# A streaming encoder step with 32 experts: two expert matrices lie over x while the experts run

## The chip, the cores and the metric

The kernel runs on one core of one Trainium2 chip. The metric is the device time of one launch in microseconds, as the median of several runs; lower is better.

## The reference

One layer of an encoder for 576 tokens of width 1024 (512 prompt rows, 64 sample rows), all in float32. In front of the mixture of experts:

```
x = x + concat(retention(q, k, v), sliding_window_attention(q, k, v)) @ w_out
hn = rmsnorm(x, norm2_g)
```

and then hierarchical experts: top-1 of 4 groups, top-2 of the 8 experts in it, 32 experts of inner width 256:

```
comb = sum(one_hot(eid, 32) * w)                 # two experts per token
for e in range(32):
    a = silu(hn @ w_gate[e]) * (hn @ w_up[e])    # 1024 -> 256
    out = out + comb[:, e:e+1] * (a @ w_down[e]) # 256 -> 1024
y = x + out                                      # x with its residual, once more
```

Each of the 96 expert matrices is 1 MiB. So 100.7 MB of weights are read, whatever the tokens choose.

## The kernel before, in words

**Stages.** Input projection, attention and retention, and output projection run up to about 320 us of the span. They are ordered by a list of steps (`plan()`). The last two blocks of that list are the output projection (w_out, two halves of 512 columns), whose results VectorE adds to `x_sb`, the tile [128, 5, 1024] that holds x with its residual in five token tiles. Beside each finished tile, ScalarE issues a DMA that writes it to DRAM, to `hn_d` (L1504, semaphore `hn_out`), and squares it for the second norm (`sq2`); TensorE transposes it for the router (L1106, `hT_ps`). Then the router picks experts on VectorE.

**Experts.** They are done in 16 pairs. For pair p, GpSimd gathers the tokens' rows from `hn_d` with an indirect DMA (L833, `xg_in`), TensorE transposes them (`rows_T`, L1156), computes gate and up for both experts (`gate_up`, L1162; pair 0 has a loop of its own, L1250), and after the activation the down product (L1177). GpSimd scatters the rows of the result to `y_d` in DRAM (L841, `y_out`). The last two pairs are not scattered; their rows are put back to tokens by one-hot products at the end.

**Weights.** SyncE (SP) issues all weight loads in the order of its program. The weights lie in a ring of 18 units of 8 KB per partition (`units`: 10 in `w_moe_a`, 8 in `w_moe_b`); one unit is one 1 MiB matrix. `gu_unit` and `dn_unit` say where the gate, up and down matrices of a pair lie. A load that reuses a unit waits until TensorE has used it: `gate_ps` and `gu_ps` count finished gate and up products, `y_ps` finished down products. Ahead of the first wait of this kind are issued gu(0), gu(1), dn(0), then (once the output projection is done, `acc_done`) gu(2), dn(1) and the first expert of gu(3): 18 units. The pair 15 (`LAST`) has its gate and up loaded in two halves (L729).

**The end.** Once the scatters are in DRAM, SP loads for each token tile the two rows of each token from `y_d` (`y_tok`, L756, over ring units that are free by then). VectorE adds the first to `x_sb` (`row_in`, L2043), TensorE or VectorE the second, TensorE adds the last two pairs (`last_rows`, L1223 and L1224), VectorE adds the sum to `x_sb` (L2088), and SP writes the output. `lows(1)` (L2035) splits the last pair's result for these products; VectorE does it behind `row_in` of tiles 0 and 1.

**Memory.** Tiles opened in a `with ... pass` block lie at the place of what is allocated next: so `x_sb` (20 KB per partition) lies over `sqT`, `probs` and others, which are in use in the attention stage only; `x_sb` is loaded again after it.

Of the kernel before, what the change touches and what calls it, by code (L numbers as in the profile page):

```python
# [14 lines left out]
P = 128  # L15
D = 1024
# [17 lines left out]
FF = 256  # L34
UNITS_A, UNITS_B = 10, 8
NUNIT = UNITS_A + UNITS_B
FIN_UNIT, OVER_UNIT, YTOK_UNIT = 12, 6, 6
LAST = NPAIR - 1
YOUT = [16 * (NPAIR // 2 - 1)] * 2
FIN_BANKS = [4, 0, 6, 2, 4]  # L40
# [158 lines left out]
def out_rows(t):  # L199
    return P if t < TAIL else DEC  # L200
# [66 lines left out]
def stream_step(nc, consts, x_prompt, x_sample, cache_ret_state, cache_swa_k, cache_swa_v,  # L267
# [20 lines left out]
    with ExitStack() as ctx:  # L288
        def sb(name, shape, dt=F32):
            return ctx.enter_context(nc.sbuf_tensor(name, shape, dt))  # L290
# [15 lines left out]
        with nc.sbuf_tensor("x_sb", [P, NT, D], F32) as x_sb:  # L306
            pass

        sqT = sb("sqT", [P, DEEP, 4, P])
        probs = sb("probs", [P, DEEP, 2, KEYS])  # L310
        probsT = sb("probsT", [P, DEEP, 2, 2, P])
# [84 lines left out]
        glu_flat = glu[:, :, :].rearrange("p a n -> p (a n)")  # L396


        w_moe_a = sb("w_moe_a", [P, UNITS_A, KD * FF])

        with nc.sbuf_tensor("units_ahead", [P, FIN_UNIT - UNITS_A, KD * FF], F32):
            with nc.sbuf_tensor("y_last", [P, 2, 2, D], F32R) as y_last:
                with nc.sbuf_tensor("oh_last", [P, 2, NT, P], F32R) as oh_last:
                    pass
        w_moe_b = sb("w_moe_b", [P, UNITS_B, KD * FF])
        rows = sb("rows", [P, 2, D])
        xg = rows
# [4 lines left out]
        actT = sb("actT", [P, 2, P])  # L412

        def gu_unit(p, e):
            return (0 if p == 0 else 6 * p - 2 if p < LAST else 6 * p) + 2 * e

        def gu_at(p, e, m):

            return 2 * m + e if p == 0 else gu_unit(p, e) + m

        def dn_unit(p, e):
            return (6 * p + 8 if p < LAST - 1 else 6 * p + 4) + e

        def units(i, n):
            i %= NUNIT
            return w_moe_a[:, i:i + n, :] if i < UNITS_A else w_moe_b[:, i - UNITS_A:i - UNITS_A + n, :]

        tmp_k = glu_flat[:, 0:2 * NT * NE].rearrange("p (k t e) -> p k t e", k=2, t=NT)
        r32 = glu_flat[:, 2 * NT * NE:3 * NT * NE].rearrange("p (t g e) -> p t g e", t=NT, g=NG)
# [21 lines left out]
        def y_tok(t, k):  # L451
            n = 2 * t + k
            return units(YTOK_UNIT + n // 2, 1)[:, 0, n % 2 * D:n % 2 * D + D]
# [163 lines left out]
        def _(sp):  # L617
# [28 lines left out]
            def load_gu_of(p, e):  # L646
                for m, v in enumerate((gate_v, up_v)):
                    sp.dma_start(units(gu_at(p, e, m), 1)[:, 0, :], v[2 * p + e]).then_inc(gu_in[p % 4], 16)  # L648
# [4 lines left out]

            def load_dn(p):
                for e in range(2):
                    sp.dma_start(units(dn_unit(p, e), 1)[:, 0, :], down_v[2 * p + e]).then_inc(dn_in[p % 4], 16)  # L656

            n_id = at["ident"][1]
            sp.dma_start(cst[:, 0:n_id], consts[:, 0:n_id]).then_inc(id_in, 16)
# [40 lines left out]
            for k in range(4, KD):  # L700
                load_weights(OUT1, k)
            load_gu(1)
            load_dn(0)


            sp.wait_ge(acc_done, NJ)
            load_gu(2)
            load_dn(1)
            for p in range(3, LAST):
                for e in range(2):  # L710
                    if p > 3:
                        sp.wait_ge(gu_ps, p - 2)
                    elif e:
                        sp.wait_ge(gate_ps, 1)
                    load_gu_of(p, e)
                if p > 3:
                    sp.wait_ge(y_ps, p - 3)
                else:
                    sp.wait_ge(gu_ps, 1)
                load_dn(p - 1)  # L720

            sp.wait_ge(gu_ps, LAST - 2)
            load_dn(LAST - 1)
            sp.wait_ge(y_ps, LAST - 3)
            for half, landed in enumerate((first_half, gu_in[LAST % 4])):
                ks = slice(half * 4 * FF, half * 4 * FF + 4 * FF)
                for e in range(2):
                    for m, v in enumerate((gate_v, up_v)):
                        sp.dma_start(units(gu_unit(LAST, e) + m, 1)[:, 0, ks], v[2 * LAST + e][:, ks]  # L729
                                     ).then_inc(landed, 16)  # L730
            sp.wait_ge(gu_ps, LAST - 1)
            load_dn(LAST)

            sp.wait_ge(slots_ready, 1)
            n_most = sp.value_load(most_i[0:1, 0:1], min_val=0, max_val=T_TOK)
# [149 lines left out]
        def _(pe):  # L885
# [284 lines left out]
                    l = nc.tensor.transpose(side3[:, P * j:P * j + P], av[:, j, :], ident)  # L1170
                return l

            def down(at_e):
                for n in range(2):
                    for j in range(2):
                        for e in range(2):
                            l = mm(acc[64 * e:64 * e + 64, 2 + n, :], actT[:, j, 64 * e:64 * e + 64],  # L1177
                                   units(at_e[e], 1)[:, 0, j * D + n * 512:j * D + n * 512 + 512],
                                   start=(j == 0), stop=(j == 1))
                return l  # L1180

# [16 lines left out]
            def down_last(q):  # L1198

                p = LAST - 1 + q  # L1200
                pe.wait_ge(aT_ev, p + 1)
                pe.wait_ge(dn_in[p % 4], p // 4 * 32 + 32)
                if q:
                    pe.wait_ge(yl_hi, 2)
                    pe.wait_ge(yl_lo, 2)
                else:
                    pe.wait_ge(y_ev, p)
                for n in range(2):
                    for j in range(2):
                        for e in range(2):  # L1210
                            l = mm(acc[64 * e:64 * e + 64, 2 + n, :], actT[:, j, 64 * e:64 * e + 64],
                                   units(dn_unit(p, e), 1)[:, 0, j * D + n * 512:j * D + n * 512 + 512],
                                   start=(j == 0), stop=(j == 1))
                    l.then_inc(y_ps, 1)

# [12 lines left out]
            def down_of(p):  # L1228
                pe.wait_ge(aT_ev, p + 1)
                pe.wait_ge(dn_in[p % 4], p // 4 * 32 + 32)  # L1230
                if p:
                    pe.wait_ge(y_ev, p)
                down([dn_unit(p, e) for e in range(2)]).then_inc(y_ps, 1)

            pe.wait_ge(idx_ready, 1)

# [30 lines left out]
            with pe.If(n_most > CAP):  # L1267
                pe.wait_ge(yl_hi, 2)
                pe.wait_ge(yl_lo, 2)

                pe.sem_inc(L_xt, 1)
                pe.sem_inc(L_y, 1)
                with pe.Fori(1, LEVELS) as lv:
                    pe.wait_ge(L_oh, lv)
                    find_rows(0, pair_dst, row_oh)
                    find_rows(32, pair_wr, row_oh.bitcast(F32)).then_inc(L_ips, 1)
                    with pe.Fori(0, NPAIR) as p:
                        it = (lv - 1) * NPAIR + p
                        pe.wait_ge(L_xg, it * 16 + 16)
                        rows_T(0).then_inc(L_xt, 1)  # L1280
                        pe.wait_ge(L_xe, it + 1)
                        pe.wait_ge(L_w, it * 96 + 96)
                        gate_up(0, (OVER_UNIT, OVER_UNIT + 2), 0).then_inc(L_gu, 1)
                        pe.wait_ge(L_act, it + 1)
                        act_T().then_inc(L_at, 1)
                        pe.wait_ge(L_ae, it + 1)
                        pe.wait_ge(L_ye, it + 1)
                        down((OVER_UNIT + 4, OVER_UNIT + 5)).then_inc(L_y, 1)
                pe.wait_ge(L_ye, NPAIR * (LEVELS - 1) + 1)

            def second_row(i):
# [284 lines left out]
        def _(dve):  # L1576
# [6 lines left out]
            def step(ins):  # L1583

                ins.then_inc(dve_step, 1)
                steps[0] += 1
                dve.wait_ge(dve_step, steps[0])
# [452 lines left out]
            def row_in(t, k):  # L2040
                R = out_rows(t)
                dve.wait_ge(yg_in[t], 32)
                step(tt(x_sb[0:R, t, :], x_sb[0:R, t, :], y_tok(t, k)[0:R, :], ALU.add))  # L2043

            n_most = dve.value_load(most_i[0:1, 0:1], min_val=0, max_val=T_TOK)
# [97 lines left out]
```

## Time and profile before

| | us |
|---|---|
| median of 3 runs | 604.15 |
| lowest and highest run | 602.49, 605.76 |
| the profiled execution's own time | 599.2 |
| its span in the trace | 597.4 |

The profile is of one execution. TensorE is busy in 87% of the span, VectorE in 41%, ScalarE in 24%, GpSimd in 25%. 144.75 MB move, 242 GB/s over the span. The page cuts the span in 40 slices of 14.9 us and gives the busy share of each engine in tenths, the clock that TensorE was granted, and the share and rate of the 16 DMA engines. q1 is the DMA queue of the SP-issued loads, q0 that of GpSimd (gathers and scatters), q10 that of ScalarE.

### The profile page before, as it was taken

Reading aid. Unit: us, or ns where it says so; the run is one execution under the profiler, and the core shown is the slowest. Engines: PE = TensorE matmul, PEld = TensorE weight load, DVE = VectorE, ACT = ScalarE, POOL = GpSimd, SP = SyncE. Lnnn points to the kernel's source line nnn. Section 1 sums busy time; section 2 is a strip of 40 time slices with the busy share of each in tenths; the row PEclk is TensorE's granted clock in tenths of the full one; section 3 lists DMA queues with packets and bytes.
Section 4 is the critical chain, followed back from the end, with each engine's and each line's share of the span. In section 5 each row is a group of like instructions: output and inputs, shape, how many; then the busy total and the mean of one; then the engine's idle time right before and its main releaser. Section 6 shows DMA issues by size and latency. Waiting matters only on the chain.

```text
span 597.4 us, 7906 instructions
## 1 busy us (share of the span) xinstructions
PE 517.0 (87%) x2938; PEld 324.1 (54%) x2938; DVE 246.2 (41%) x576; ACT 144.6 (24%) x364; POOL 151.1 (25%) x287
## 2 busy tenths in 40 slices
PE   3597998999999999889995499999978787778895
PEld 3584776777777677568784463334333332333343
DVE  2857668869432465651225522122211101111337
ACT  4542344444635222232111100011000000000110
POOL 5064646203304444651102111111211101100000
PEclk9887997999999999999997589999988988888999
DMA  8521030022005922246926949999999999999884
GB/s 248 206 61 43 19 116 27 2 71 71 2 16 168 320 114 72 70 153 234 418 83 243 420 164 408 412 424 424 425 423 426 425 427 424 425 425 421 363 331 169
DMA packets 35031, 144.75 MB, mean 242 GB/s; under 512 B 5842, under 2 KB 8994, under 8 KB 23216
## 3 DMA queue, kind: packets, MB, share of 16 engines
q1 hardware_dynamic: 27440, 131.58, 55.9%
q0 software_dynamic: 4528, 9.01, 4.2%
q10 hardware_dynamic: 3024, 3.64, 1.8%
q8 instruction: 24, 0.39, 0.3%
q14 instruction: 15, 0.12, 0.1%
HBM read 138.16 MB, written 17.30 MB: 260 GB/s over the span
## 4 chain that ended last, share of the span: by engine, by line
PE 45%; SPq 21%; DVE 15%; issue 5%; ACT 4%; DMA 3%; POOL 2%; ACTq 0%; DVEq 0%; POOLq 0%
PE banks L940 18%; SPq L648 12%; PE banks L1162 7%; SPq L656 6%; DMA w_moe_a<-in_w_up_dram 3%; SPq L729 3%; PE banks L1177 3%; PE banks L1156 2%; PE banks L1115 1%; POOL w_lo L795 1%; PE banks L998 1%; PE banks L1083 1%; PE banks L1078 1%; DVE soft L1720 1%; PE banks L1250 1%
## 5 line engine op out<-in xcount | busy, mean ns | idle before, releaser
L795 POOL TENSOR_TENSOR w_lo<-w_raw,w_hi 128x512 fp32r<-128x512 f32 x52 | 69.1, 1347 | 124.1 <-ACT w_hi L1408 122.4
L1162 PE MATMUL banks<-w_moe_b,xgT 128*64 128x512 f32 x224 | 70.9, 659 | 16.4 <-DMA w_moe_b<-in_w_up_dram 10.5
L1162 PE MATMUL banks<-w_moe_a,xgT 128*64 128x512 f32 x224 | 68.1, 631 | 8.9 <-DMA w_moe_a<-in_w_up_dram 8.9
L940 PE MATMUL banks<-w_hi,xT_hi_a 128*128 128x512 f32 (+4 forms) x140 | 56.6, 404 | 7.0 <-ACT sv L1376 7.0
L1990 DVE SCALAR_TENSOR_TENSOR glu<-banks,wr,glu 128x256 f32<-128x256 f32 x15 | 7.3, 483 | 122.8 <-ACT glu L1537 122.8
L841 POOL DMA_INDIRECT y_d<-y_sb,idx x14 | 14.1, 1005 | 166.7 <-PE banks L1156 111.1
L940 PE MATMUL banks<-w_lo,xT_hi_a 128*128 128x512 f32 (+4 forms) x140 | 53.9, 385 | 0.0
L940 PE MATMUL banks<-w_hi,xT_lo_a 128*128 128x512 f32 (+4 forms) x140 | 53.6, 383 | 0.0
L1162 PEld LDWEIGHTS banks<-w_moe_b,xgT 128*64 128x64 f32 x224 | 22.4, 152 | 57.4 <-issue 54.7
L1537 ACT ACTIVATE glu<-banks,wr 128x256 f32<-128x256 f32 x15 | 7.1, 475 | 155.2 <-PE banks L1162 137.5
L940 PE MATMUL banks<-w_hi,xT_hi_b 128*128 128x512 f32 (+3 forms) x100 | 41.6, 416 | 0.4 <-POOL w_lo L795 0.4
L1954 DVE TENSOR_TENSOR xgT<-banks,g_both 128x1024 f32<-128x1024 f32 x16 | 19.6, 1225 | 53.2 <-PE banks L1156 53.2
L940 PE MATMUL banks<-w_lo,xT_hi_b 128*128 128x512 f32 (+3 forms) x100 | 39.5, 395 | 0.0
L940 PE MATMUL banks<-w_hi,xT_lo_b 128*128 128x512 f32 (+3 forms) x100 | 39.2, 392 | 0.0
L1162 PEld LDWEIGHTS banks<-w_moe_a,xgT 128*64 128x64 f32 x224 | 21.6, 146 | 31.1 <-issue 30.8
L1408 ACT CAST w_hi<-w_raw 128x512 fp32r<-128x512 f32 x52 | 30.6, 615 | 14.6 <-DMA w_raw<-in_w_out_dram 9.0
L1177 PE MATMUL banks<-w_moe_a,actT 128*64 128x512 f32 x144 | 32.6, 593 | 1.4 <-DVE actT L2007 1.4
L940 PEld LDWEIGHTS banks<-w_hi,xT_hi_a 128*128 128x128 f32 (+2 forms) x140 | 26.1, 187 | 13.4 <-ACT sv L1376 7.2
L1452 ACT ACTIVATE probs<-banks,soft,rstd_qk 128x208 f32<-128x208 f32 (+1 forms) x40 | 20.6, 519 | 52.4 <-DVE soft L1725 52.4
L940 PEld LDWEIGHTS banks<-w_hi,xT_lo_a 128*128 128x128 f32 (+2 forms) x140 | 25.9, 185 | 6.1
L940 PEld LDWEIGHTS banks<-w_lo,xT_hi_a 128*128 128x128 f32 (+2 forms) x140 | 26.1, 187 | 4.7
L833 POOL DMA_INDIRECT rows<-hn_d,idx x16 | 16.3, 1022 | 37.5 <-PE banks L1156 23.4
(273 smaller groups left out, 888.7 us busy)
## 6 DMA issues: line engine op xcount, KB each, us to landing
w_moe_a<-in_w_down_dram SPq DMA_DIRECT2D x20, 1024.0 KB, 25.5
w_moe_a<-in_w_gate_dram SPq DMA_DIRECT2D x16, 1024.0 KB, 18.6
w_moe_a<-in_w_up_dram SPq DMA_DIRECT2D x16, 1024.0 KB, 21.5
w_moe_b<-in_w_gate_dram SPq DMA_DIRECT2D x14, 1024.0 KB, 24.1
w_moe_b<-in_w_up_dram SPq DMA_DIRECT2D x14, 1024.0 KB, 25.8
w_moe_b<-in_w_down_dram SPq DMA_DIRECT2D x12, 1024.0 KB, 24.8
w_raw<-in_w_in_dram SPq DMA_DIRECT2D x36, 256.0 KB, 4.6
y_d<-in_consts_dram SPq DMA_DIRECT2D x9, 512.0 KB, 10.3
```

The source lines that it names most:

```text
L648: sp.dma_start(units(gu_at(p, e, m), 1)[:, 0, :], v[2 * p + e]).then_inc(gu_in[p % 4], 16)
L656: sp.dma_start(units(dn_unit(p, e), 1)[:, 0, :], down_v[2 * p + e]).then_inc(dn_in[p % 4], 16)
L729: sp.dma_start(units(gu_unit(LAST, e) + m, 1)[:, 0, ks], v[2 * LAST + e][:, ks]).then_inc(landed, 16)
L795: nc.gpsimd.tensor_tensor(w_lo[:, s, :], w_raw[:, s, :], w_hi[:, s, :].bitcast(F32), ALU.subtract).then_inc(split, 1)
L833: pool.indirect_dma_start(out=xg[:, u, :], out_offset=None, in_=hn_d, in_offset=bass.IndirectOffsetOnAxis(ap=idx[:, p:p + 1], axis=0), bou ...
L841: pool.indirect_dma_start(out=y_d, out_offset=bass.IndirectOffsetOnAxis(ap=idx[:, NPAIR + p:NPAIR + p + 1], axis=0), in_=y_sb[:, u, :], in ...
L940: l = mm(acc2[0:R, j % 2, 0:width], a[:, P * t:P * t + R], w, start=(kk == 0 and q == 0), stop=(kk == KD - 1 and q == 2))
L1162: l = mm(acc[64 * e:64 * e + 64, u, :].rearrange("p (m f) -> p m f", m=2), xgT[:, xu, k, 64 * e:64 * e + 64], units(at_e[e], 2)[:, :, k * ...
L1177: l = mm(acc[64 * e:64 * e + 64, 2 + n, :], actT[:, j, 64 * e:64 * e + 64], units(at_e[e], 1)[:, 0, j * D + n * 512:j * D + n * 512 + 512] ...
L1408: nc.scalar.copy(w_hi[:, s, :], w_raw[:, s, :]).then_inc(hi_done, 1)
L1452: af(probs[0:R, q, hl, :], sideA[0:R, b, 256 * hl:256 * hl + KEYS], ACT.Exp, scale=rstd_qk[0:R, h + hl:h + hl + 1], bias=soft[0:R, q, 2 + ...
L1954: tt(xgT[:, u], at[:, 0:2, :].rearrange("p b (j n) -> p (b j) n", j=4), g2T.unsqueeze(2).to_broadcast([P, KD, P]), ALU.mult).then_inc(xg_e ...
```

## The change

Three things:

- A tile `w_moe_x` of two units lies over `x_sb`. The down matrices of pair 0 go there, once nothing reads `x_sb` any more (writes to `hn_d` landed, router transposes and squares done). The ring of 18 units is numbered anew without them: dn(1) takes the place of dn(0), and 20 units are issued ahead of the first wait on the experts' products. dn(3) is issued behind `gu_ps` 1.
- Behind the last weights, SP reads x from `hn_d` back to `x_sb`, five DMAs that wait for nothing (576 rows of 4 KB). `row_in` waits for them.
- The one-hot tile of the last pairs (`oh_last`) moves to unit 4, and the order and waits of the last loads follow the new places: dn(14) waits for `y_ps` 12 and stands before the wait on `gu_ps` 13; dn(15) waits for `y_ps` 13.

```diff
+        with nc.sbuf_tensor("w_moe_x", [P, 2, KD * FF], F32) as w_moe_x:
+            pass
...
         def gu_unit(p, e):
-            return (0 if p == 0 else 6 * p - 2 if p < LAST else 6 * p) + 2 * e
+            return max(6 * p - 2, 0) + 2 * e
...
-        def dn_unit(p, e):
-            return (6 * p + 8 if p < LAST - 1 else 6 * p + 4) + e
+        def dn_at(p, e):
+            return w_moe_x[:, e, :] if p == 0 else units(6 * p + 2 + e, 1)[:, 0, :]
...
             load_gu(1)
-            load_dn(0)
+            load_dn(1)
             sp.wait_ge(acc_done, NJ)
             load_gu(2)
-            load_dn(1)
-            for p in range(3, LAST):
-                for e in range(2):
-                    if p > 3:
-                        sp.wait_ge(gu_ps, p - 2)
-                    elif e:
-                        sp.wait_ge(gate_ps, 1)
-                    load_gu_of(p, e)
-                if p > 3:
+            sp.wait_ge(hn_out, 16 * NT)
+            sp.wait_ge(hT_ps, 2 * NT)
+            sp.wait_ge(sq2, 2 * NT)
+            load_dn(0)
+            load_gu_of(3, 0)
+            load_dn(2)
+            sp.wait_ge(gate_ps, 1)
+            load_gu_of(3, 1)
+            sp.wait_ge(gu_ps, 1)
+            load_dn(3)
+            for p in range(4, LAST):
+                sp.wait_ge(gu_ps, p - 2)
+                load_gu(p)
+                if p > 4:
                     sp.wait_ge(y_ps, p - 3)
-                else:
-                    sp.wait_ge(gu_ps, 1)
-                load_dn(p - 1)
+                    load_dn(p - 1)
+            sp.wait_ge(y_ps, LAST - 3)
+            load_dn(LAST - 1)
             sp.wait_ge(gu_ps, LAST - 2)
-            load_dn(LAST - 1)
-            sp.wait_ge(y_ps, LAST - 3)
             for half, landed in enumerate((first_half, gu_in[LAST % 4])):
...
-            sp.wait_ge(gu_ps, LAST - 1)
+            sp.wait_ge(y_ps, LAST - 2)
             load_dn(LAST)
+            for t in range(NT):
+                n = out_rows(t)
+                sp.dma_start(x_sb[0:n, t, :], hn_d[P * t:P * t + n, :]).then_inc(x_in[t], 16)
...
             def row_in(t, k):
                 dve.wait_ge(yg_in[t], 32)
+                dve.wait_ge(x_in[t], 48 if t < TAIL else 64)
```

## Rows read from the trace of the kernel before

**Rows 1.** The page's second part: DMA rate in 40 slices of the span.
```profile
GB/s 248 206 61 43 19 116 27 2 71 71 2 16 168 320 114 72 70 153 234 418 83 243 420 164 408 412 424 424 425 423 426 425 427 424 425 425 421 363 331 169
```

**Rows 2.** The chain of waits: start us, us, what.
```profile
425.05 5.97 SPq L648
...
549.44 18.14 DMA w_moe_a<-in_w_up_dram
```

**Rows 3.** Windows: us, busy us (instructions) of PE, PEld, DVE, ACT, POOL, PEclk, DMA share, GB/s.
```profile
302.00:306.00 4.00, 4.00 (x24) 3.43 (x23) 1.57 (x3) 0.00 (x0) 0.00 (x0) 1.00 0.00 0
318.80:343.40 24.60, 8.94 (x47) 8.32 (x47) 15.52 (x55) 3.92 (x7) 6.55 (x15) 0.56 0.96 384
345.00:349.00 4.00, 4.00 (x20) 3.67 (x21) 1.40 (x2) 0.00 (x0) 0.99 (x1) 0.50 0.00 0
...
377.60:424.00 46.40, 46.40 (x230) 17.93 (x228) 10.10 (x16) 5.94 (x8) 8.11 (x8) 1.00 1.02 423
424.00:560.00 136.00, 110.00 (x490) 44.65 (x488) 22.41 (x40) 13.38 (x18) 14.14 (x14) 0.91 1.01 424
564.00:570.00 6.00, 4.91 (x24) 1.61 (x22) 0.44 (x1) 0.00 (x0) 0.00 (x0) 1.00 0.46 186
```

**Rows 4.** Timeline of SP: start us, us, its DMA issues.
```profile
318.76 0.33 SPq L648 DMA_DIRECT2D w_moe_b<-in_w_gate_dram  x1
...
352.57 0.33 SPq L648 DMA_DIRECT2D w_moe_a<-in_w_gate_dram  x1
...
364.21 0.67 SPq L648 DMA_DIRECT2D w_moe_a<-in_w_up_dram  x1
...
377.61 0.33 SPq L648 DMA_DIRECT2D w_moe_b<-in_w_gate_dram  x1
...
569.22 3.90 SPq L756 DMA_DIRECT2D w_moe_a<-y_d  x8
```

**Rows 5.** Landing of L648's loads issued at 322-324, 352-354, 362-366, 377-380.
```profile
DMA to landing us min/median/max: 18.2/19.5/20.7
...
DMA to landing us min/median/max: 4.8/5.9/6.9
...
DMA to landing us min/median/max: 5.4/9.4/14.2
...
DMA to landing us min/median/max: 8.8/12.9/17.1
```

**Rows 6.** Landing: last `hn_d` write (319.5); gather issued 338.3; the gathers after 352.
```profile
DMA to landing us min/median/max: 9.0/9.0/9.0
...
DMA to landing us min/median/max: 6.7/6.7/6.7
...
DMA to landing us min/median/max: 10.1/10.5/10.7
```

**Rows 7.** Queue of GpSimd from 399 to 404: packets, MB, share of 16 engines.
```profile
q0 software_dynamic: 224, 0.46, 23.3%
```

**Rows 8.** Timeline of PE: start us, us, instructions, [idle before].
```profile
345.13 3.65 PE L1156 MATMUL banks<-cst,rows 128*128 128x128 f32 x16
...
429.82 7.09 PE L1162 MATMUL banks<-w_moe_a,xgT 128*64 128x512 f32 x32 [0.43 <-DMA w_moe_a<-in_w_up_dram]
...
445.83 9.85 PE L1162 MATMUL banks<-w_moe_b,xgT 128*64 128x512 f32 x32 [4.17 <-DMA w_moe_b<-in_w_up_dram]
...
479.36 8.45 PE L1162 MATMUL banks<-w_moe_a,xgT 128*64 128x512 f32 x32 [5.07 <-DMA w_moe_a<-in_w_up_dram]
```

**Rows 9.** Timeline of DVE at the end.
```profile
575.00 1.23 DVE L2043 TENSOR_TENSOR x_sb<-x_sb,w_moe_a 128x1024 f32<-128x1024 f32 x1 [1.15 <-DMA w_moe_a<-y_d]
577.82 1.22 DVE L2043 TENSOR_TENSOR x_sb<-x_sb,w_moe_a 128x1024 f32<-128x1024 f32 x1 [1.59 <-DMA w_moe_a<-y_d]
579.07 1.29 DVE L2035 TENSOR_TENSOR y_last<-banks,y_last 128x512 fp32r<-128x512 f32 x2
581.70 1.22 DVE L2088 TENSOR_TENSOR x_sb<-x_sb,banks 128x1024 f32<-128x1024 f32 x1 [1.34 <-PE banks L1224]
```

More of the change, by code:

```diff
@@ L36 @@
 NUNIT = UNITS_A + UNITS_B
-FIN_UNIT, OVER_UNIT, YTOK_UNIT = 12, 6, 6
+FIN_UNIT, OVER_UNIT, YTOK_UNIT, OH_UNIT = 12, 6, 6, 4
 LAST = NPAIR - 1
@@ L396, in stream_step @@
         glu_flat = glu[:, :, :].rearrange("p a n -> p (a n)")
+        with nc.sbuf_tensor("units_ahead_oh", [P, OH_UNIT, KD * FF], F32):
+            with nc.sbuf_tensor("oh_last", [P, 2, NT, P], F32R) as oh_last:
+                pass
         w_moe_a = sb("w_moe_a", [P, UNITS_A, KD * FF])
@@ L402, in stream_step @@
             with nc.sbuf_tensor("y_last", [P, 2, 2, D], F32R) as y_last:
-                with nc.sbuf_tensor("oh_last", [P, 2, NT, P], F32R) as oh_last:
-                    pass
+                pass
         w_moe_b = sb("w_moe_b", [P, UNITS_B, KD * FF])
@@ L655, in load_dn @@
                 for e in range(2):
-                    sp.dma_start(units(dn_unit(p, e), 1)[:, 0, :], down_v[2 * p + e]).then_inc(dn_in[p % 4], 16)
+                    sp.dma_start(dn_at(p, e), down_v[2 * p + e]).then_inc(dn_in[p % 4], 16)
             n_id = at["ident"][1]
@@ L1171, in act_T, with down @@
                 return l
-            def down(at_e):
+            def down(mats):
                 for n in range(2):
@@ L1177, in down @@
                             l = mm(acc[64 * e:64 * e + 64, 2 + n, :], actT[:, j, 64 * e:64 * e + 64],
-                                   units(at_e[e], 1)[:, 0, j * D + n * 512:j * D + n * 512 + 512],
+                                   mats[e][:, j * D + n * 512:j * D + n * 512 + 512],
                                    start=(j == 0), stop=(j == 1))
@@ L1211, in down_last @@
                             l = mm(acc[64 * e:64 * e + 64, 2 + n, :], actT[:, j, 64 * e:64 * e + 64],
-                                   units(dn_unit(p, e), 1)[:, 0, j * D + n * 512:j * D + n * 512 + 512],
+                                   dn_at(p, e)[:, j * D + n * 512:j * D + n * 512 + 512],
                                    start=(j == 0), stop=(j == 1))
@@ L1232, in down_of @@
                     pe.wait_ge(y_ev, p)
-                down([dn_unit(p, e) for e in range(2)]).then_inc(y_ps, 1)
+                down([dn_at(p, e) for e in range(2)]).then_inc(y_ps, 1)
             pe.wait_ge(idx_ready, 1)
@@ L1287, in _ @@
                         pe.wait_ge(L_ye, it + 1)
-                        down((OVER_UNIT + 4, OVER_UNIT + 5)).then_inc(L_y, 1)
+                        down([units(OVER_UNIT + 4 + e, 1)[:, 0, :] for e in range(2)]).then_inc(L_y, 1)
                 pe.wait_ge(L_ye, NPAIR * (LEVELS - 1) + 1)
```

## The prediction, made before the result was known

> **What bounds the kernel now.** I read the slices of the page first, then the chain of waits, then windows, and last the issues and landings of single loads. The slices show a rate that falls to 2 to 83 GB/s in places up to 358 us (24 slices of 14.9 us), and then 408 to 427 GB/s for thirteen slices [rows 1]. The chain of waits says the same: from 425 us to 549 us it runs over SP's load issues, and then over one load that lands 18.14 us after its issue, at 567.6 [rows 2]. The windows give the detail: 423 and 424 GB/s from 377.6 to 560, a flat line, while TensorE is busy 110.0 of 136.0 us behind 424 [rows 3]. So the end of the stream of weights sets the end of the kernel, and it can come earlier only if DMA time that is idle now is used for weights. There is such time: nothing moves from 302 to 306 and from 345 to 349 [rows 3]. The second hole is there because the ring of 18 units is full until TensorE has used its first units; SP goes on at 352.57 [rows 4].
>
> **What the two extra units can bring.** Before, eight units are issued from 318.76 on and the last lands at 322.7 + 20.7 = 343.4 [rows 4, 5], 24.6 us for 8.4 MB of weights and the rest, 384 GB/s [rows 3]. The change issues ten there. At 424 GB/s a unit of 1.049 MB takes 2.47 us, so two take 4.95 us, and the last lands at about 348.4, still ahead of 352.57. dn(0), gu(3) and dn(2) must wait for the last write to `hn_d`, which lands at 319.5 + 9.0 = 328.5 [rows 6]. Queued ahead of them is gu(2), 4.2 MB or 9.9 us, and the writes' own bytes beside it, until about 331; so this wait leaves the engines no hole. If it came 2 us late, the cover up to 352.57 would still hold it. Behind this wait on SP stand only loads that TensorE wants later than pair 0's gate and up (dn(0) first).
>
> So 4.95 us of loads move into the hole. But the ring behind it is not larger. I counted the units that may be issued by the wait on `gu_ps` 3, at 377.61 [rows 4]: before 18 + 2 + 2 + 4 + 2 = 28, after 20 + 2 + 2 + 4 = 28, and from there on both kernels have the same waits in the same order up to dn(13). The gain is thus what the queue is behind at 377.61, and no more. Before, the first load issued there lands 8.8 us later; a load that finds the queue empty lands in 4.8 us [rows 5]. The queue is 4.0 us behind. Cross-check: after, the last of the eight units issued from 352.57 is the load issued at 364.21, which lands at 364.2 + 14.2 = 378.4 [rows 4, 5] just as before; its transfer is over some 2 us ahead of that, so the queue is empty at 377.61. **The lead is 4.0 us, not 4.95**, if TensorE reaches `gu_ps` 3 at the same time. After 377.61 TensorE runs 230 products in 46.4 us [rows 3], 58 of which make a pair (32 + 16 + 8 + 2), so each pair frees six units in 11.7 us and they take 14.8 us to load, so the lead stays to the end of the stream.
>
> **What fills the hole is in the way of the gathers.** TensorE transposes the rows of pairs 0 and 1 from 345.13 on, 3.65 us for both, so it wants the second gather at 345.13 + 1.82 = 346.95 [rows 8]. This gather is issued at 338.3 and lands 6.7 us later, at 345.0 [rows 6], because the weights ahead of it run dry at 343.4. All gathers timed after 352, with weights in the queue all along, land after 10.1 to 10.7 us [rows 6]. With the change the weights go on to 348.4, so I take 10.4 us: 348.7, and TensorE waits 1.75 us. Bounds: 0 (it lands as now) and 338.3 + 10.7 - 346.95 = 2.05. gate_up(0) stands behind that wait, and all that frees ring units behind it, so the lead shrinks by as much: SP issues gu(5) at 379.4 instead.
>
> Here the Trainium skill has a rule against the row. "DMA: Bandwidth & Descriptors", section "Queues, rings and completion order", says that each engine goes round the queues that have work, a packet at a time. By equal turns the gathers' queue would get up to half of the engines, a gather and a scatter together (0.46 MB, [rows 7]) would be through in 2.2 us at 212 GB/s, and there would be no stall. The trace doesn't agree with equal shares: with weights beside it the GpSimd queue has 23.3% of the engines' time [rows 7]. I go by the landings.
>
> **The clock.** From 345 to 349 the granted clock is 0.50, the 1.2 GHz level [rows 3], and it rises to 2.4 GHz behind this stretch, in which TensorE is busy throughout (4.00 of 4.00 us). A stall of 1.75 us in this stretch may put the rise off. What a start at the low level costs is seen later: after a wait of 4.17 us a pair takes 9.85 us, after 5.07 us 8.45 us, against 7.09 us at the high level [rows 8], so 1.4 to 2.8 us lost, which is a low stretch of 2.7 to 5.5 us. Here the second transposes (1.8 us, low anyway) take the first part of it. What is left costs (2.7 - 1.8) / 2 = 0.45 to (5.5 - 1.8) / 2 = 1.9 us; 0 if the rise comes as before. I take 0.4. The lead is then 4.0 - 1.75 - 0.4 = 1.85 us, bounds 0.05 and 4.0.
>
> **What reading x back costs.** 576 x 4096 B = 2.36 MB, 5.6 us at 424 GB/s, queued behind dn(15) and ahead of the `y_tok` loads, which SP issues when the last scatter has landed (569.22, [rows 4]). Cover: from 564 to 570 the engines are 46% busy at 186 GB/s [rows 3], so (424 - 186) x 6 us = 1.4 MB of the read fit in. But those 46% (seven engines of sixteen on average, the scatter's share among them) are engines that end late. I estimate that some five still have weights until shortly before 570 and the others are done at about 564. A load has landed only when its share on every engine has. On the late engines x takes its 5.6 us from about 569.7 to 575.3, the two loads of tile 0 another 2.5 us, and the receipt about 0.7: 578.5. Now VectorE gets them at 575.0 and those of tile 1 at 577.8 [rows 9]; after, 578.5 and 581.0 (all this on a clock shifted by the lead). `lows(1)` stands behind `row_in(1)` on VectorE: 579.07 now [rows 9], 582.3 then. TensorE has other products until 581.7, so last_rows(0, 1), which needs it, ends at 584.0 instead of 581.6, and the chain of VectorE adds that begins at 581.70 [rows 9] begins 2.4 us later. Bounds: 0 (the idle engines cover it all) and 5.6 (no cover). I take 2.4.
>
> The Trainium skill says why the slowest engine counts: "DMA: Bandwidth & Descriptors", section "Why a DMA increments its semaphore by 16 and not by 1", has a load's engines finish on their own, and only the full count says that all has landed. By that rule the cost is 2.4 us, by the mean of the engines (idle 1.4 of 2.36 MB) it would be near 1. No row here shows one engine alone.
>
> **At nothing:** the wait of `row_in` on `x_in` (x lands ahead of the `y_tok` loads in the same queue); dn(14) waiting for `y_ps` 12 and dn(15) for `y_ps` 13 (SP's issues run some ten units, over 20 us, ahead of the landings there, and the product waited for has been done; if one of them did hold SP, it would cost what it exceeds that); `oh_last` at another place; TensorE reading dn(0) from elsewhere.
>
> **Sum.** -1.85 + 2.4 = +0.55 us on the profiled execution's 599.2 us (span 597.4): 599.75. The median of the runs shown, 604.15, is 4.95 above that execution; I carry the difference over: **604.7 us**. About 0.5%, 3.0 us, is what a measurement of this kernel can tell from no change.
>
> **The rivals.**
> - *The hole is free and x is covered.* Lead 4.0 and x read for 0.5: -3.5 us, 600.65. For it: holes in rows 3, and the idle engines. Against it: the landings of the gathers. Chance 0.20.
> - *Only the gathers are unharmed* (equal turns of the queues, the rule above, or a second gather that gets through as the first): lead 4.0, x 2.4, so -1.6 us, 602.55. Chance 0.15.
> - *The end pays for x in full.* The read stands in one queue ahead of loads that the last adds wait for; if the late engines decide and VectorE's row of adds has no slack, 5.6 us are paid against a lead of 1.85: +3.75 us, 607.9. It decides once the read costs 3.0 us more than the lead brings. For it: VectorE waits for `y_d` twice at the end [rows 9]. Against: 54% idle engines in 564 to 570. Chance 0.25.
> - *It doesn't do what it says:* if the queue was dry at 377.61 anyway, the lead is 0 and the time 606.5; the 8.8 us speak against it, and it is within my forecast's 0.40.
>
> **How the numbers follow.** Forecast 0.40, with the rivals 0.20, 0.15 and 0.25. Faster by over 0.5%: the first rival, 0.20. Slower: the third, 0.25. Same: 0.55. Range: from the full lead and x for nothing (600.2) to a lead of about 1 and x at 5.6 (608.8).
>
> **What would show it.** Right: last load ahead of TensorE's first products lands at 348 to 349; the second gather lands over 9 us after its issue and the second transposes start at 348 to 349; gu(5)'s first load lands near 384.5, not 386.4; the last half of gu(15) lands 1 to 3 us earlier; x lands at 572 to 575 and `row_in(1)` begins about 1.3 us later than now. Wrong: no wait ahead of the second transposes, or `row_in` on time, or a stream that ends over 4 us early.

## The result, and the profile after

The kernel after takes 612.09 us (median of 4 runs, 610.51 to 613.97), the kernel before in the same session 603.32 us (601.48 to 605.76). The ratio is 1.0153, with a 95% interval of 1.0121 to 1.0184: the change costs 9 us where 0.55 were forecast, and the time lies above the range.

The profiled execution has a span of 612.1 us and a time of 613.97. The two traces don't run on one clock: SP's first issue behind `acc_done` is at 318.76 before and at 322.35 after. That is the scatter of executions and not the change, since kernels with the head of before have it too (318.91 and 323.86 in two runs below). I call this issue t0 and compare from there: the last instruction ends 278.6 us behind it before and 289.8 after, so 11.2 us have come in, and the stretches behind t0 show where. (By the medians it is 9: the execution that was profiled before, at 599.2 us, is a short one of its kernel. Differences between two single traces carry such scatter.) The page's rates first, against [rows 1].

```profile
GB/s 253 189 68 40 13 138 2 2 70 70 2 64 189 313 36 71 69 234 245 346 70 339 420 199 396 354 422 421 423 422 427 424 428 421 427 424 420 356 243 162
```

The middle is as flat as before. A slice of 354 GB/s stands at its beginning, where before had 412, and the last but one has 243 for 331. SP's issues, against [rows 4]: t0, dn(0) to its own place, `gu_ps` 3, the five reads of x and the `y_tok` loads.

```profile
322.35 0.33 SPq L653 DMA_DIRECT2D w_moe_b<-in_w_gate_dram  x1
...
332.04 0.80 SPq L661 DMA_DIRECT2D w_moe_x<-in_w_down_dram  x2
...
385.09 0.33 SPq L653 DMA_DIRECT2D w_moe_b<-in_w_gate_dram  x1
...
559.60 7.89 SPq L745 DMA_DIRECT2D x_sb<-hn_d  x5
572.66 6.14 SPq L769 DMA_DIRECT2D w_moe_a<-y_d  x8
```

`gu_ps` 3 comes at t0 + 62.74; before it came at t0 + 58.85. The whole lead is gone here, 3.9 of 4.0 us. PE's timeline tells why, against [rows 8]; the last line is from the end of the kernel.

```profile
348.95 1.97 PE L1169 MATMUL banks<-cst,rows 128*128 128x128 f32 x8 [0.24 <-DMA rows<-hn_d,idx]
352.38 1.97 PE L1169 MATMUL banks<-cst,rows 128*128 128x128 f32 x8 [1.46 <-DMA rows<-hn_d,idx]
354.28 9.19 PE L1263 MATMUL banks<-w_moe_a,xgT 128*64 128x256 f32 x64
...
588.64 3.78 PE L1308 MATMUL banks<-w_moe_a,cst 128*128 128x512 f32 x4 [4.05 <-DMA w_moe_a<-y_d]
```

The second gather holds TensorE for 1.46 us, the first for 0.24. Pair 0's gate and up then begin at t0 + 31.93 (before 29.95) and take 9.19 us where they took 7.26: 2.0 us from the gathers, 1.9 us from the clock, which the windows show still at 0.50 while those products run.

```profile
348.60:352.60 4.00, 2.30 (x10) 1.79 (x10) 1.22 (x1) 0.00 (x0) 0.91 (x1) 0.50 0.85 353
354.00:356.00 2.00, 2.00 (x10) 1.00 (x10) 1.58 (x3) 0.00 (x0) 0.88 (x1) 0.50 0.21 72
567.60:573.60 6.00, 3.42 (x18) 1.11 (x16) 0.06 (x1) 0.00 (x0) 0.00 (x0) 0.99 0.98 397
576.00:582.00 6.00, 5.50 (x24) 2.48 (x22) 1.39 (x3) 0.47 (x1) 0.00 (x0) 0.92 1.02 289
```

The hole is filled as meant: 348.6 to 352.6 lies as far behind t0 as 345 to 349 does before, and has 353 GB/s where [rows 3] have 0. So is the idle part: 567.6 to 573.6 answers to 564 to 570 before, 397 GB/s for 186. But behind it the engines are busy at 1.02 and move only 289 GB/s. The end of VectorE, against [rows 9]:

```profile
588.62 1.23 DVE L2057 TENSOR_TENSOR x_sb<-x_sb,w_moe_a 128x1024 f32<-128x1024 f32 x1 [8.07 <-DMA w_moe_a<-y_d]
592.98 1.22 DVE L2057 TENSOR_TENSOR x_sb<-x_sb,w_moe_a 128x1024 f32<-128x1024 f32 x1 [3.13 <-DMA w_moe_a<-y_d]
594.24 1.29 DVE L2048 TENSOR_TENSOR y_last<-banks,y_last 128x512 fp32r<-128x512 f32 x2
596.41 1.22 DVE L2102 TENSOR_TENSOR x_sb<-x_sb,banks 128x1024 f32<-128x1024 f32 x1 [0.88 <-PE banks L1237]
```

Tile 0 comes at t0 + 266.3 (before 256.2), tile 1 at t0 + 270.6 (before 259.1): 10 and 11.5 us late. `y_tok` is issued as early as before (t0 + 250.3, before 250.5) and lands late. The landing of these loads, in us behind their issue, first before and then after:

```profile
DMA to landing us min/median/max: 4.4/8.2/11.3
```
```profile
DMA to landing us min/median/max: 9.0/15.5/19.7
```

Two links of the chain of waits after, the second gather and the chain's last but for what VectorE and the outputs do:

```profile
341.71 10.62 DMA rows<-hn_d,idx
...
574.78 18.12 DMA w_moe_a<-y_d
```

The trace also keeps the time at which each of the 16 shares of a load lands (the 16 steps of its semaphore), though not which engine each belongs to. The last share of dn(15), the last load of weights, lands at t0 + 253.8 before and at t0 + 255.8 after. The last share of x lands at t0 + 263.3, the last of tile 0 at t0 + 266.2. These three times are used again below.

### The profile page after: what moved, and what is told of

Same layout as the page of the kernel before. It is cut to its first block, busy times and chain, and to the rows that moved or that the text cites. A ratio compares the mean times of both kernels' runs of the same rounds, so it can differ in the third digit from the quotient of the medians.

```text
span 612.1 us, 7916 instructions
## 1 busy us (share of the span) xinstructions
PE 524.8 (86%) x2938; PEld 327.8 (54%) x2938; DVE 246.4 (40%) x576; ACT 144.8 (24%) x364; POOL 151.0 (25%) x287
## 4 chain that ended last, share of the span: by engine, by line
PE 46%; SPq 14%; DVE 13%; DMA 11%; issue 5%; ACT 3%; POOL 2%; ACTq 0%; DVEq 0%; POOLq 0%
PE banks L953 19%; SPq L653 10%; PE banks L1175 8%; DMA w_moe_b<-in_w_up_dram 5%; SPq L661 4%; PE banks L1190 3%; DMA w_moe_a<-y_d 3%; PE banks L1011 2%; DMA rows<-hn_d,idx 2%; DMA y_d<-y_sb,idx 2%; PE banks L1263 1%; PE banks L1169 1%; POOL w_lo L808 1%; PE banks L1128 1%; PE banks L1096 1%
## 5 line engine op out<-in xcount | busy, mean ns | idle before, releaser
L1175 PE MATMUL banks<-w_moe_a,xgT 128*64 128x512 f32 x224 | 70.5, 645 | 6.5 <-DMA w_moe_a<-in_w_up_dram 6.5
## 6 DMA issues: line engine op xcount, KB each, us to landing
w_moe_b<-in_w_gate_dram SPq DMA_DIRECT2D x14, 1024.0 KB, 11.2
```

What stands on the lines that cost most here:

```text
L1175: l = mm(acc[64 * e:64 * e + 64, u, :].rearrange("p (m f) -> p m f", m=2), xgT[:, xu, k, 64 * e:64 * e + 64], units(at_e[e], 2)[:, :, k * ...
```

## The experiments

Fourteen kernels ran. Ratios are to the kernel before, timed beside each on its chip, with 95% intervals; at 603 us, 0.001 is 0.6 us. First the two halves of the change, apart.

**The read-back alone** (e1): the kernel before with this behind `load_dn(LAST)`, and `row_in` waiting for it.
```
+            for t in range(NT):
+                sp.dma_start(x_sb[0:n, t, :], hn_d[P * t:P * t + n, :]).then_inc(x_in[t], 16)
+                dve.wait_ge(x_in[t], 48 if t < TAIL else 64)
```


> The kernel before with one thing added: behind the last weights SP reads x back from hn_d, and row_in waits for it (x_sb holds the same x anyway). Theory A (the read-back at the end is what costs: it keeps late DMA engines late and holds up the loads of y_d): nearly the whole of the change's 8.8 us, so 7 to 11 us slower than before, and the first y_d tile lands some 10 us later. Theory B (the stall of the gathers and the late clock cost most, the end only its 5.6 us less cover): 2 to 3 us slower.

Measured: 1.0133 (1.0103 to 1.0162), so 8.0 us. The end of VectorE (t0 is 318.91, so these times compare with [rows 9] directly):
```profile
583.63 1.23 DVE L2048 TENSOR_TENSOR x_sb<-x_sb,w_moe_a 128x1024 f32<-128x1024 f32 x1 [9.44 <-DMA w_moe_a<-y_d]
588.32 1.22 DVE L2048 TENSOR_TENSOR x_sb<-x_sb,w_moe_a 128x1024 f32<-128x1024 f32 x1 [3.47 <-DMA w_moe_a<-y_d]
```
The windows of this kernel, then the two of before that answer to 570 to 576 and 576 to 582:
```profile
564.00:570.00 6.00, 4.90 (x24) 1.63 (x22) 0.69 (x1) 0.05 (x1) 0.00 (x0) 1.00 0.95 378
570.00:576.00 6.00, 5.51 (x26) 2.44 (x24) 1.39 (x3) 0.47 (x1) 0.00 (x0) 1.00 1.00 304
576.00:582.00 6.00, 2.23 (x12) 0.49 (x8) 0.00 (x0) 1.17 (x2) 0.00 (x0) 0.93 1.03 362
582.00:588.00 6.00, 4.35 (x6) 2.19 (x7) 1.23 (x1) 0.00 (x0) 0.00 (x0) 0.50 0.87 213
```
```profile
570.00:576.00 6.00, 5.51 (x24) 2.36 (x22) 2.39 (x4) 0.47 (x1) 0.00 (x0) 1.00 0.98 353
576.00:582.00 6.00, 6.00 (x24) 3.06 (x21) 3.04 (x5) 1.17 (x2) 0.00 (x0) 1.00 1.04 406
```
In 564 to 570 the rate is 378 instead of 186 GB/s: 1.15 MB more, close to the 1.4 MB of my estimate, and still tile 0 is 8.5 us late (t0 + 264.7). The idle engines did take their share, and it brought nothing. The end of this trace is 11.6 us behind that of before; the medians say 8.0.

**The head alone** (e2): the kernel after without the read; `x_sb` is set to zero, so x is left out of the result.
```
-                sp.dma_start(x_sb[0:n, t, :], hn_d[P * t:P * t + n, :]).then_inc(x_in[t], 16)
+            nc.gpsimd.memset(x_sb[:, :, :], 0.0).then_inc(rows_clear, 1)
```


> The changed kernel without the read-back: GpSimd sets x_sb to zero behind its last scatter instead, so x is left out of the result. The early loads are as in the changed kernel. Theory A: the lead of 4.0 us is eaten by the late second gather (about 1.8 us) and the late clock (about 1.9 us), so within 1 us of before. Theory B: still 5 us or more slower than before.

Measured: 1.0034 (1.0004 to 1.0065), 2.0 us slower. The second gather is late again:
```profile
349.52 1.97 PE L1166 MATMUL banks<-cst,rows 128*128 128x128 f32 x8 [1.76 <-DMA rows<-hn_d,idx]
```
The waits for weights in pairs 8 to 11 stand at t0 + 127.2, 143.8, 160.8 and 178.0 (before 127.1, 143.7, 160.6, 177.7): no lead. 8.0 + 2.0 is the 9.2 of the whole, within the intervals. In the trace of after, the same waits stand at t0 + 128.5, 145.1, 162.0 and 179.1, 1.4 us behind before. But the first of them lies anywhere from 126.5 (e6) to 128.9 (e7) in traces whose head is that of before, so one trace doesn't tell a lead of 0 from a loss of 1.4 us.

**dn(2) held back until both gathers are in** (e3), in the kernel after:
```
             load_gu_of(3, 0)
+            sp.wait_ge(xg_in[0], 16)
+            sp.wait_ge(xg_in[1], 16)
             load_dn(2)
```


> The changed kernel, with dn(2) issued only when the first two gathers have landed. If the two extra units are what makes the second gather late: it lands after under 8 us instead of 10.6, pair 0 starts 2 us earlier and at the full clock, the lead of 4 us is there, and the kernel is about 4 us faster than the changed one (608). If the gather is late for another reason: no faster than the changed one (612).

**The same without the read** (e11; x left out as in e2).

> The changed kernel with dn(2) held back until the rows of pairs 0 and 1 have landed, and without the read-back (x is left out of the result, x_sb is set to zero). It is the head of the change alone with the gathers unharmed. The theory that the lead is what the queue was behind at gu_ps 3 gives 4.0 us: 599.0 where before has 603.0, ratio 0.993. The theory that only 1 MB of the two units got ahead (as the bytes moved in the run with the hold and the read showed) gives 2 to 2.5 us: ratio 0.996. If the stream isn't what sets the end, ratio 1.000.

Measured: e3 1.0141 (1.0109 to 1.0174), e11 0.9955 (0.9931 to 0.9979). In both the rows are transposed without a wait; here e3:
```profile
348.94 3.65 PE L1171 MATMUL banks<-cst,rows 128*128 128x128 f32 x16
```
e11 is the head as it could be. Its gu(5) lands from t0 + 64.3 (before 67.7), the last load of gu(14) at t0 + 224.1 (before 227.1), the last share of dn(15) at t0 + 250.9 (before 253.8), and the kernel gains 2.7 us (1.3 to 4.2). So a lead of 3 to 3.4 us exists and lasts. Against e2, which differs from it in the hold alone, e11 is 4.8 us faster: the stall and the clock that the traces price at 3.9 us. e3 missed its expectation of 4 us below after (it is 0.7 below), although its gathers were on time. Its waits for weights in pairs 8 to 11 stand where before has them (t0 + 127.1 to 177.7; e11 has 125.0 to 175.6), its last load of gu(14) was 1.2 us early, and its last share of dn(15) came at t0 + 254.6. e3 and e11 differ in the read alone, yet lie 11.2 us apart, more than any other run with the read and its partner. Why the lead was lost in e3 the traces don't tell.

**Where the read stands.** e4 is the kernel after with x(t) read tile by tile ahead of its own two `y_tok` loads; e8 the same with the hold of e3 and without tile 4, whose x was never overwritten.
```
             for t in range(NT):
                 n = out_rows(t)
+                sp.dma_start(x_sb[0:n, t, :], hn_d[P * t:P * t + n, :]).then_inc(x_in[t], 16)
                 for k in range(2):
```


> The changed kernel, with x read back behind the wait on the last scatter and tile by tile ahead of its two y_d loads (x 0, y 0, y 0, x 1, ...). If the order and the late engines cost: tile 0 is 1.3 us, tile 1 2.5 us later than in before, and the kernel is 2 to 4 us slower than before (606). If reads of hn_d and y_d next to each other are slow whatever their order: 8 us or more slower (611 and over).

> The changed kernel with three mends: dn(2) waits for the first two gathers, x is read back tile by tile between the y_d loads, and tile 4, which the two matrices don't cover, is not read. The head then costs nothing against before and the end what e4 showed: 2 to 3 us slower than before. If the lead of the two early units reaches the end of the stream (4 us by the prediction), 1 to 2 us faster than before.

**Read in mid-stream** (e9): the hold, and tiles 0 to 3 read behind dn(4).
```
                     load_dn(p - 1)
+                if p == 5:
+                    for t in range(TAIL):
+                        sp.dma_start(x_sb[:, t, :], hn_d[P * t:P * t + P, :]).then_inc(x_in[t], 16)
```


> As e8, but the four tiles of x are read in the middle of the stream of weights, behind dn(4), once pair 0's down product is done. If the stream is bound by bytes on every engine: 2.1 MB cost 5 us at its end, less the lead, and nothing behind it, so 3 to 5 us slower than before. If the stream has slack that the late engines don't show: no slower than before.

**Split** (e12): as e8, but tiles 0 and 1 are read behind dn(15).

> The changed kernel with dn(2) held back, tile 4 not read, x of tiles 0 and 1 read behind dn(15) and x of tiles 2 and 3 behind the y_tok loads of tiles 0 and 1. Against the run in which all four were interleaved (ratio 1.0032): if the idle engines before the last scatter lands take the first two tiles, they come for nothing and tile 0 and 1 are on time, so 2 us less, ratio 0.998 to 1.000; if every byte ahead of y_tok is paid, tile 0 is 2 us later than in that run and the end the same or 1 us later, ratio 1.003 to 1.006.

Measured: e4 1.0087 (1.0055 to 1.012), e8 1.0032 (1.0009 to 1.0056), e9 1.0040 (1.0019 to 1.0062), e12 1.0038 (1.0017 to 1.006). Interleaving saves 4 us of the 9. Tile 0 then waits for one tile of x and not for five, and comes 1.0 us later than before, tile 1 2.2 (expected 1.3 and 2.5); the kernel was expected 2 to 4 us slower and is 5.2, of which e2 has 2.0 for the head. But against e11 (0.9955), which doesn't read, the three with the hold are 4.6, 5.1 and 5.0 us slower. 2.10 MB at 424 GB/s are 4.95 us. At these three places the bytes of x are paid about once (each of the differences is good to some 2 us). Read ahead of every `y_tok` load they cost more: 8.0 us in e1, 7.2 in after against e2, 11.2 in e3 against e11, for 5.6 us of bytes. The expectation that the first two tiles come for nothing in e12 was wrong. e8 keeps the lead (its last share of dn(15) lands at t0 + 250.5), for which 1 to 2 us faster than before was expected, and is 1.9 us slower; e9 was expected 3 to 5 us slower and is 2.4. No complete kernel of these beats the one before. A read behind the `y_tok` loads, with the adds in another order, wasn't tried.

**When and from where.** e6 is the kernel before with the read issued only when the last weights have landed; e7 is e1 with the rows read from the inputs instead of `hn_d` (what the attention added to x is left out of the result).
```
+            sp.wait_ge(gu_in[LAST % 4], LAST // 4 * 64 + 64)
+            sp.wait_ge(dn_in[LAST % 4], LAST // 4 * 32 + 32)
```


> As e1_read_only (the kernel before plus the read-back), but SP issues the read only once the last weights have landed, so all engines begin x together. Theory A (the read-back costs that much because it is queued while some engines still have weights: the lateness is handed on to the y_d loads, and packets get slower): the y_d loads of tile 0 land 6 us later than in before instead of 8.6, and the kernel is 4 to 6 us slower than before, against 8.0 in e1. Theory B (the 2.4 MB are simply expensive, whenever they are read): as slow as e1 or slower, 8 to 10 us.

> As e1_read_only, but the read takes the same bytes from x_prompt and x_sample in place of hn_d (so the output has x without its residual from the first stage). If reads of hn_d are slow for where it lies, or for having been written by this kernel: the y_d loads land 3 to 4 us earlier than in e1 and the kernel is 4 to 5 us slower than before. If it is the queueing: like e1, 8 us.

Measured: e6 1.0144 (1.0112 to 1.0176), e7 1.0139 (1.0108 to 1.017). The source doesn't make the 8 us. e6 was expected 4 to 6 us slower if queueing behind the weights made them, and is 8.7 slower. It isn't a pure test of this: SP's wait for the last weights ends at t0 + 253.1, so x begins that late on the idle engines too, and SP issues the `y_tok` loads at t0 + 257.1 instead of 250.5. What it does show is that packets are slow without weights beside them. With no weights left, the windows of e6 show the slow engines again, 304 GB/s at full occupation, and 412 when the `y_tok` loads come:
```profile
582.00:588.00 6.00, 0.00 (x0) 0.00 (x0) 0.00 (x0) 0.00 (x0) 0.00 (x0) 0.57 1.02 304
588.00:590.00 2.00, 1.95 (x3) 0.92 (x4) 1.23 (x1) 0.00 (x0) 0.00 (x0) 0.50 1.00 412
```

**How much** (e10): e1 with two tiles instead of five, 1.05 MB.
```
-            for t in range(NT):
+            for t in range(2):
```


> The kernel before with the read-back behind the last weights, but of tiles 0 and 1 alone (1.05 MB of the 2.36 MB). Theory A (every byte ahead of the y_tok loads is paid, at the rate of these packets): the five tiles cost 8.0 us, so two cost 1.05 / 2.36 of it, 3.6 us, ratio 1.006, row_in(0) 3.6 to 4 us late. Theory B (the idle engines of the stretch before the last scatter lands, 186 of 424 GB/s for 6 us, take about 1.4 MB, and only what is over that is paid): two tiles cost 0 to 0.5 us, ratio 1.000. Theory C (the cost is one of being late once, a slow phase of the engines or TensorE's clock after any wait, not of bytes): 6 to 8 us again, ratio 1.010 or more.

Measured: 1.004 (1.0012 to 1.0068), 2.4 us. t0 is 324.82 here, so the first line is t0 + 259.15, 2.9 us behind before:
```profile
583.97 1.23 DVE L2049 TENSOR_TENSOR x_sb<-x_sb,w_moe_a 128x1024 f32<-128x1024 f32 x1 [4.02 <-DMA w_moe_a<-y_d]
586.52 1.23 DVE L2049 TENSOR_TENSOR x_sb<-x_sb,w_moe_a 128x1024 f32<-128x1024 f32 x1 [1.32 <-DMA w_moe_a<-y_d]
```
1.05 MB fit into the idle time easily, if idle time counted; by bytes they are 2.5 us. They are paid in full by the trace, but at the full rate and not at the slower one of e1, by which theory A gave 3.6 us. Theory B gave 0 to 0.5 us; the interval (0.7 to 4.1 us) leaves it out, if narrowly.

**Row size.** e13 reads two units of weights (2.10 MB in rows of 8192 bytes) to the place of x tiles 0 to 3, whose x is then missing from the result; e14 reads x in rows of 2048 bytes.

> The kernel before with, behind dn(15), two units of weights read into the place of x tiles 0 to 3 in x's stead (2.10 MB in rows of 8192 bytes where the read-back has 2.36 MB in rows of 4096; these tiles' x is left out of the result). Bytes alone at 424 GB/s: 4.95 us, ratio 1.008. If rows of 4096 bytes are what makes the engines fall to about 300 GB/s in the tail, this is the result, with 400 GB/s and more until the y_tok loads begin. If the fall comes from elsewhere (the engines out of step at the end of the stream, whatever is read), the cost is 7 us, ratio 1.012, and the rate falls to 300 here too.

> The kernel before with the read-back of all five tiles, as in the run of the read alone (8.0 us, ratio 1.0133), but every tile in two loads of 2048-byte rows. If the size of a row decides how slow the tail's reads are, this is worse than 8.0 us: 10 us or more, ratio 1.017 and up. If bytes and the fall of the rate whatever is read decide, 8 us again, ratio 1.013.

Measured: e13 1.0103 (1.0064 to 1.0143), e14 1.0115 (1.0074 to 1.0156). One after the other, windows 570 to 576 and 576 to 582 of e13 (t0 319.43), the same of e14 (t0 319.69), and tile 0 on VectorE in e13:
```profile
570.00:576.00 6.00, 5.51 (x26) 2.48 (x24) 1.39 (x3) 0.47 (x1) 0.00 (x0) 1.00 0.95 359
576.00:582.00 6.00, 3.94 (x18) 1.24 (x15) 0.91 (x1) 1.17 (x2) 0.00 (x0) 0.98 1.03 421
```
```profile
570.00:576.00 6.00, 5.52 (x26) 2.51 (x24) 1.39 (x3) 0.47 (x1) 0.00 (x0) 1.00 0.84 255
576.00:582.00 6.00, 3.39 (x16) 0.86 (x12) 0.00 (x0) 1.17 (x2) 0.00 (x0) 1.00 1.04 326
```
```profile
581.09 1.23 DVE L2049 TENSOR_TENSOR x_sb<-x_sb,w_moe_a 128x1024 f32<-128x1024 f32 x1 [6.09 <-DMA w_moe_a<-y_d]
```
e13's tile 0 is 5.4 us late for 4.95 us of bytes, e14's 8.9 for 5.6. With wide rows the rate is back at 421 in the second window; with rows of 4096 and 2048 it isn't. But e14's ten issues keep SP until 571.6, so its `y_tok` loads are issued at t0 + 253.6, 3.1 us later than before, and part of its low rate (0.84 of the engines' time) is engines that have nothing to do. e14 isn't worse than e1, as a rule by row size would have it, e10 reads rows of 4096 bytes at nearly the full rate on its slowest engine (2.6 us for 2.5, below), and the intervals of e1, e13 and e14 overlap. This stays inconclusive.

**Less in the stream** (e5): the kernel before with the loads of dn(8) cut to one sixteenth, 1.97 MB less (that pair's down products use stale data).
```
+                    w = 128 if p == 8 else 2 * D
```


> The kernel before with the loads of dn(8) cut to one sixteenth of their columns (the rest of that pair's down matrices is stale): 1.97 MB less in the middle of the stream. If the stream is bound by bytes at 424 GB/s from 377.6 us to its end, this brings 4.6 us: ratio 0.992. If the lead of a stream is lost on the way (other waits, a stretch bound by TensorE), 0 to 2.5 us: ratio 0.996 to 1.000.

Measured: 0.9945 (0.9922 to 0.9969), 3.3 us of the 4.6 that the bytes are. The last share of dn(15) lands at t0 + 250.1, 3.7 us earlier than before. The stream does set the end, and a little is lost on the way.

**The last shares, side by side**, in us behind t0. The fourth column is the time from the last share of dn(15) to the last of x; I take both to be of one engine, the slowest, which the trace doesn't name.

| | dn(15) | x | between | tile 0 | bytes of x at 424 GB/s |
|---|---|---|---|---|---|
| before | 253.8 | | | 256.2 | |
| e1 | 254.6 | 262.1 | 7.5 | 264.7 | 5.6 |
| after | 255.8 | 263.3 | 7.5 | 266.2 | 5.6 |
| e7 | 256.1 | 263.4 | 7.3 | 267.5 | 5.6 |
| e14 | 255.1 | 262.7 | 7.6 | 265.1 | 5.6 |
| e10 | 253.8 | 256.4 | 2.6 | 259.1 | 2.5 |
| e13 | 254.2 | 259.2 | 5.0 | 261.6 | 4.95 |

In e1 the first share of the last tile of x lands at t0 + 249.1, before SP has issued a `y_tok` load, and the last 13 us later. For the early engines the idle time covers x wholly, for the slowest one not at all.

## Why the prediction was wrong

**The step that failed is the cost of reading x back: 2.4 us, "bounds: 0 (...) and 5.6 (no cover)". It costs 8.0 us (e1).** Two things were wrong in it.

First the cover. The idea was sound that the engines which end late decide; the error is the estimate that they are through with the weights at about 569.7. In the trace of before the last packet of weights ends at t0 + 253.4, which is 572.2, and the last share of dn(15) lands at 572.6, 14 us behind the first. So 2.5 us of the cover weren't there. No row of the prediction shows this; [rows 9] has tile 0 at 575.0, but its loads are issued at 569.22, and their shares on the other engines land up to 574.3 as well. All of x then stands between the slowest engine's weights and tile 0, and idle engines elsewhere cover nothing. The runs agree: 1.05 MB cost 2.9 us at tile 0 (e10) and 2.10 MB 5.4 (e13), each near the time of the bytes, though in e1 1.15 MB more moved in 564 to 570. The packets' records show the same spread: in e1 SP's queue moves many packets of x from t0 + 246 on (84 of 4096 bytes in 2 us, where before has 12), and the last of the weights' packets of 8192 bytes start at t0 + 252 to 254. On the bytes alone the third rival (5.6 us, paid in full) was the right account, and I gave it 0.25.

Its rule in the Trainium skill, "DMA: Bandwidth & Descriptors", section "Why a DMA increments its semaphore by 16 and not by 1", that only the full count says that all of a load has landed, is borne out by the traces: the shares of one tile of x land 13 us apart in e1, VectorE starts with the last share of its loads, and in e10 idle engines took 1.05 MB and the tile was late by all of it.

Second the rate. The upper bound took 424 GB/s for granted. In e1 the engines move 304 GB/s in 570 to 576 and 362 in 576 to 582, occupied at 1.00 and 1.03; before has 353 and 406 there. The records of single packets say the same: one of 4096 bytes takes 159 ns in the stream, and 208 to 229 ns on the mean in t0 + 252 to 258. An engine has 36 such packets of x: 5.7 us at 159 ns, and the 7.5 us of the slowest engine are 208 ns each, 1.9 us more than the bytes at 424 GB/s. At tile 0 the forecast of 3.5 us (578.5 for 575.0), the 2.5 us of cover, these 1.9 and the 0.8 us by which e1's weights end later make 8.7, where e1 has 8.5; and 7.5 lies within the interval of e1's 8.0 (6.2 to 9.7). The 1.1 us that the prediction took off between tile 0 and the end don't show in e1's trace, where the end is 11.6 us late. Why packets slow down is open: not the source (e7), not the weights beside them (e6), and the row size isn't settled (e10, e13, e14).

**The lead.** "The lead is 4.0 us, not 4.95": right in kind. With the gathers unharmed gu(5) lands 3.4 us early and the kernel gains 2.7 (e11). That the second gather is late was right in size: 10.62 us from issue to landing against 10.4, 1.46 + 0.24 us of waits and a start of the products 2.0 us late against 1.75. The last extra load landed at t0 + 31.0, which is 349.8 on before's clock, against 348.4. The prediction held its row of shares against equal turns of the queues. That reading was too strong, and so would it be here, where in 342 to 350 the weights' queue (first line: packets, MB, share) has 81.7% of the engines and GpSimd's 19.5%:

```profile
q1 hardware_dynamic: 383, 2.76, 81.7%
q0 software_dynamic: 230, 0.63, 19.5%
```

The gathers have no packet on the engines before 344. A packet of theirs is one row of 4096 bytes and takes 159 ns, one of the weights 8192 bytes and 309 ns, so by turns of one packet each they would get a third of the time and not half. From 345 to 346 the trace has 39 packets of rows beside 32 of weights, from 346 to 348 41 beside 81. So the stall of the gathers doesn't refute equal turns, and doesn't prove them; the estimate of 2.2 us, which rests on the half, was too short. The landings, by which the prediction went, were right.

**The clock.** "I take 0.4": wrong by 1.5 us. Pair 0's gate and up took 1.9 us longer, the upper bound; e2 has 7.88 us there, and e11, in which TensorE doesn't wait, 7.13. In sum 3.9 us of delay stand against a lead of 4.0, and `gu(5)`'s first load landed at t0 + 67.8, as before (67.7), not at 65.7. The forecast lead of 1.85 was 0.1. That the slow products are the stall's doing is shown by e11, where it is gone and they take 7.13 us. So the head alone should cost nothing; e2 measured 2.0 us (0.2 to 3.9), and its profiled execution, one of its shortest, shows no such loss (its last instruction ends at t0 + 278.3, before's at 278.6). That difference stays open.

**At nothing:** nothing in the traces speaks against these. SP's issues of dn(14) and dn(15) run ahead of their landings as before.

**The sum.** Forecast -1.85 + 2.4; measured, +2.0 for the head (a lead of 0.1 left, by the trace of after) and +8.0 for the read, 9.2 for both at once. None of the rivals gave this. The largest, "the end pays for x in full", ended at +3.75, with the lead overrated by 1.75 and the read underrated by 2.4. Of the signs, the late gather came; `gu(5)` near 384.5, an earlier gu(15), x at 572 to 575 (it landed at t0 + 263.3, 582.1 on before's clock) and a `row_in(1)` 1.3 us late (11.5) did not. None of the three signs that were named as "wrong" would have told of this outcome.

## What to carry to other kernels

A read queued ahead of the loads that the end waits for costs at least its whole bytes, even when half the engines are idle by the mean: take the time at which the slowest engine comes free from the last share of the last load ahead of the read (here 14 us behind the first), not from the occupation of a window. Space bought with bytes that must be read again is worth it only if the read has idle time of its own: here 2.10 MB moved into a hole brought 2.7 us at best, and reading as much back cost 5 us at three places (all 2.36 MB ahead of every `y_tok` load: 8). Filling a hole also takes it from the transfers that live in it; the gathers, and behind them the clock, took the lead back to the last 0.1 us.

## What the runs showed of the hardware

- DMA engines can be occupied at 1.00 to 1.03 and move 304 GB/s (e1) or 289 (after), where the stream has 424. The share of busy time doesn't show it, the rate does.
- At the end of the stream the shares of the same two loads, dn(15), land from t0 + 239.7 to 253.8 before and from 239.4 to 254.6 in e1. A load queued behind them inherits that spread: in e1 13 us for each tile of x.
- After 1.46 us of wait the granted clock stayed at the 1.2 GHz level for part of the products behind it: 9.19 us instead of 7.26. At the end a wait of 4.05 us let four products of `second_row` take 3.78 us, which take 1.99 before; in e1 the windows show 0.50 from 582 to 588.
